# A transformer block on one core: the expert router fed with the sums ahead of the norm, and the second chunk's last norm pass on ScalarE and GpSimd

## The reference, cut to what matters

```python
mix = jnp.concatenate([ret_o, swa_o, mla_o], axis=-1) @ w_out[l]
x = layer_norm(DEEPNORM_ALPHA * x + mix, ln1_g[l], ln1_b[l])
# layer_norm: (xf - mu) * rsqrt(var + LN_EPS) * g + b
ffn = grouped_moe(x, router_w, router_bias, exp_w_gate_up[l], exp_w_down[l])
# grouped_moe: scores = sigmoid(x @ router_w)                      16 experts
#   biased = scores + router_bias; the best of 4 groups (sum of its top 2),
#   then the top 2 experts inside it; gates = their normalised scores
#   h = x @ w_gate_up[e]; a = silu(h[:256]) * h[256:] * gate; y += a @ w_down[e]
x = layer_norm(DEEPNORM_ALPHA * x + ffn, ln2_g[l], ln2_b[l])
```

## Time and profile before

| | us |
|---|---|
| median of 3 runs | 1554.58 (1554.37 to 1555.19) |
| the profiled execution, its own time | 1554.16 |
| its span, first to last instruction | 1552.3 |
| mean granted TensorE clock | 0.998 of full |
| TensorE busy | 1525.1, 98% |
| VectorE busy | 835.7, 54% |
| ScalarE busy | 710.5, 46% |
| POOL busy | 88.8, 6% |

### The profile page before, as it was taken

How to read it: one execution, slowest core, us unless ns; L and a number is a source line. 1 busy time by engine, 2 the same in 40 slices (tenths; PEclk the granted TensorE clock), 3 DMA queues, 4 the chain that set the end, 5 groups by cost and what they waited for, 6 DMA issues and landing times.

```text
span 1552.3 us, 20392 instructions
## 1 busy us (share of the span) xinstructions
PE 1525.1 (98%) x7476; PEld 1167.2 (75%) x7476; DVE 835.7 (54%) x1126; ACT 710.5 (46%) x1179; POOL 88.8 (6%) x159
## 2 busy tenths in 40 slices
PE   8999999999999999999999999999999999999998
PEld 7886445877443788888888888878888888888886
DVE  4675215476422755546667555565555556755544
ACT  5662123674212544446474444453444537554443
POOL 2420000140000000002000000000000010000000
PEclk9999999999999999999999999999999999999999
DMA  7537997546699655566345655546555653655551
GB/s 247 204 135 296 372 421 294 173 142 279 248 421 414 220 184 192 183 207 199 115 156 170 210 191 183 186 152 208 185 185 191 208 164 109 203 190 189 189 189 56
DMA packets 165986, 328.30 MB, mean 211 GB/s; under 512 B 8874, under 2 KB 106896, under 8 KB 152992
## 3 DMA queue, kind: packets, MB, share of 16 engines
q1 hardware_dynamic: 164992, 323.52, 59.5%
q0 software_dynamic: 928, 3.89, 0.8%
HBM read 326.33 MB, written 1.05 MB: 211 GB/s over the span
## 4 chain that ended last, share of the span: by engine, by line
PE 90%; DVE 3%; DMA 3%; ACT 2%; issue 1%; DVEq 1%; POOL 0%; SPq 0%; POOLq 0%; ACTq 0%
PE bank L449 23%; PE bank L451 23%; PE bank L450 23%; PE bank L1221 6%; PE bank L1267 3%; DMA sb_raw<-w_in 2%; PE bank L853 1%; PE bank L1180 1%; PE bank L1181 1%; DMA sb_raw<-ffn_w 1%; PE bank L1275 1%; PE bank L1276 1%; DVE sb_wlo L445 1%; PE bank L930 1%; PE bank L882 1%; ACT sb_whi L438 1%
## 5 line engine op out<-in xcount | busy, mean ns | idle before, releaser
L445 DVE TENSOR_TENSOR sb_wlo<-sb_raw,sb_whi 128x1024 fp32r<-128x1024 f32 (+2 forms) x419 | 483.3, 1197 | 347.4 <-ACT sb_whi L438 347.0
L438 ACT ACTIVATE sb_whi<-sb_raw 128x1024 fp32r<-128x1024 f32 (+2 forms) x419 | 408.0, 1027 | 322.1 <-PE bank L451 303.6
L449 PE MATMUL bank<-sb_whi,sb_op_hi 128*128 128x512 f32 (+2 forms) x1216 | 475.3, 391 | 6.5 <-DVE sb_op_lo L2012 3.5
L451 PE MATMUL bank<-sb_whi,sb_op_lo 128*128 128x512 f32 (+2 forms) x1216 | 467.8, 385 | 0.0
L450 PE MATMUL bank<-sb_wlo,sb_op_hi 128*128 128x512 f32 (+2 forms) x1216 | 467.1, 384 | 0.0
L449 PEld LDWEIGHTS bank<-sb_whi,sb_op_hi 128*128 128x128 f32 x1216 | 228.7, 188 | 53.3 <-issue 4.3
L451 PEld LDWEIGHTS bank<-sb_whi,sb_op_lo 128*128 128x128 f32 x1216 | 228.6, 188 | 46.1
L450 PEld LDWEIGHTS bank<-sb_wlo,sb_op_hi 128*128 128x128 f32 x1216 | 228.9, 188 | 42.6
L449 PE MATMUL bank<-sb_whi,sb_lat_hi 128*128 128x512 f32 (+2 forms) x456 | 175.7, 385 | 1.0 <-DVE sb_wlo L445 1.0
L451 PE MATMUL bank<-sb_whi,sb_lat_lo 128*128 128x512 f32 (+2 forms) x456 | 174.5, 383 | 0.0
L450 PE MATMUL bank<-sb_wlo,sb_lat_hi 128*128 128x512 f32 (+2 forms) x456 | 174.4, 382 | 0.0
(11 more groups left out here) (269 smaller groups left out, 1337.3 us busy)
## 6 DMA issues: line engine op xcount, KB each, us to landing
sb_raw<-ffn_w SPq DMA_DIRECT2D x264, 512.0 KB, 4.3
sb_moe<-exp_w_gate_up SPq DMA_DIRECT2D x46, 1024.0 KB, 9.7
sb_raw<-w_in SPq DMA_DIRECT2D x84, 512.0 KB, 4.6
sb_moe<-exp_w_down SPq DMA_DIRECT2D x26, 1024.0 KB, 10.0
sb_raw<-w_out SPq DMA_DIRECT2D x32, 512.0 KB, 4.4
sb_per_block<-exp_w_gate_up SPq DMA_DIRECT2D x8, 1024.0 KB, 7.0
sb_xT<-exp_w_gate_up SPq DMA_DIRECT2D x6, 1024.0 KB, 10.2
sb_xg<-exp_w_gate_up SPq DMA_DIRECT2D x4, 1024.0 KB, 8.9
```

Of the source, the lines that this page charges most:

```text
L438: nc.scalar.activation(h, r, ACT.Copy).then_inc(hi_made.sem, 1)
L445: nc.vector.tensor_tensor(o, r, h.bitcast(F32), ALU.subtract).then_inc(lo_made.sem, 1)
L449: nc.tensor.matmul(ps, hi, wh, start=first, stop=False)
L451: return nc.tensor.matmul(ps, lo, wh, start=False, stop=last)
```

## The change

- The router no longer reads the normed x. ScalarE copies the four finished sums out of their banks (`sums_out`) into `sums_of` (in the memory that was unused under xs_lo), and TensorE transposes those; chunk 0's transposes stand ahead of the last product group. VectorE's statistics wait for ScalarE's copy of the same half.
- The norm is put into the router weights instead, once in layer 0. With W' = g * W, centred over the 1024 rows, and t = sum of b * W over the rows, the logits are rstd * (sums @ W') + t. g and b of both layers come with the small vectors (two more DMAs, 102 columns in place of 70), VectorE makes the four products and their partial sums, a TensorE matmul with ones adds them over the partitions, and VectorE centres the two weight sets (they lie in `poolw`, which is loaded only in the second model).
- All four copies into xT are ScalarE's. The scaling by rstd and t is two small VectorE operations (`logits`) ahead of the sigmoid.
- The second norm pass of chunk 1 is split: ScalarE multiplies by rstd (`scaled`), POOL adds b. POOL also makes one of the four xs_lo halves. The order of the xs_hi copies, residual matmuls and filler is changed.

```diff
@@ POOL, routing stage @@
                     nc.gpsimd.tensor_tensor(lrstd[:, n % 2:n % 2 + 1], lve[:, n % 2:n % 2 + 1], half[:, 0:1], ALU.pow).then_inc(F["ln_rstd"].sem, 1)
+                    if n == 1:
+                        for nh in range(2):
+                            v, cols_of = x[:, 1, 512 * nh:512 * nh + 512], slice(512 * nh, 512 * nh + 512)
+                            pool.wait_ge(F["normed"].sem, F["normed"].after(l, nh + 1))
+                            nc.gpsimd.tensor_tensor(v, v, table[:, 1, cols_of], ALU.add).then_inc(F["ln1"].sem, 1)
+                        pool.wait_ge(F["xs_hi"].sem, F["xs_hi"].after(l, 1))
+                        lo, hi = (t[:, 0, 4:8, :] for t in (xs_lo, xs_hi))
+                        v = x[:, 0, 512:1024].rearrange("p (q j) -> p j q", j=4)
+                        nc.gpsimd.tensor_tensor(lo, v, hi.bitcast(F32), ALU.subtract).then_inc(F["xs_lo0"].sem, 1)
@@ TensorE @@
+                if l == 0:
+                    pe.wait_ge(rw_summed.sem, 1)
+                    nc.tensor.matmul(bank[4][:, 0:2 * DEPTH * NE], c("ones"), rw_sums, start=True, stop=True).then_inc(rw_total.sem, 1)
                 for ch in range(NC):
                     for nh in range(2):
                         if ch == 0:
                             slab_ready(num(S1_OUT + 2 + nh))
+                        elif nh == 1:
+                            if l == 0:
+                                pe.wait_ge(rw_centred.sem, 1)
+                            routing_transposes(0)
...
-                routing_transposes(0)
+                routing_transposes(1)
                 router(0)
+                router(1)
+                fold(0)
+                fold(1)
+                wait(F, "ln1", l, 2)
                 open_residual(0)
-                routing_transposes(1)
-                fold(0)
-                router(1)
-                fold(1)
-                open_residual(1)
-                kept_busy(3, 512, const[:, 0:512])
+                wait(F, "ln1", l, 3)
+                open_residual(1, (0,))
+                kept_busy(1, 512, const[:, 0:512])
...
                 count(bank[5][:, 0:NE], ones).then_inc(F["counted"].sem, 1)
-                kept_busy(1, 512, const[:, 0:512], 7)
+                wait(F, "ln1", l, 4)
+                open_residual(1, (1,))
@@ ScalarE @@
                 nc.scalar.preload_act_table(ACT.Sigmoid)
+                sums_out(0, 0)
+                sums_out(0, 1)
+                sums_out(1, 0)
                 routing_out(0)
                 routing_out(1)
+                sums_out(1, 1)
+                routing_out(2)
+                routing_out(3)
                 logit_out(0)
+                logit_out(1)
+                wait(F, "scaled", l, 1)
+                scaled(0)
+                wait(F, "logits", l, 1)
+                nc.scalar.activation(scores, biased, ACT.Sigmoid).then_inc(F["routed"].sem, 1)
+                scaled(1)
+                wait(F, "ln1", l, 2)
                 token_hi(0)
-                routing_out(2)
-                logit_out(1)
-                wait(F, "folded", l, 2)
-                nc.scalar.activation(scores.rearrange("p c e -> p (c e)"), bank[5][:, 0:32], ACT.Sigmoid).then_inc(F["routed"].sem, 1)
+                wait(F, "ln1", l, 4)
                 token_hi(1)
@@ VectorE, start of layer 0 @@
+                    for i, weighed in enumerate((rw_g, rw_b)):
+                        for n in range(DEPTH):
+                            o = COLS + DK * (DEPTH * i + n)
+                            tt(weighed[n], rw_tiles, bank[7][:, o:o + DK].unsqueeze(2).to_broadcast([P, DK, NE]), ALU.mult)
+                    dve.drain()
+                    for n, t in enumerate((*rw_g, *rw_b)):
+                        i = nc.vector.tensor_reduce(rw_sums[:, NE * n:NE * n + NE], t.rearrange("p k e -> p e k"), axis=AX.X, op=ALU.add)
+                    i.then_inc(rw_summed.sem, 1)
@@ VectorE, routing stage @@
+                if l == 0:
+                    dve.wait_ge(rw_total.sem, 1)
+                    for n in range(DEPTH):
+                        stt(out=rw_g[n], in0=bank[4][:, NE * n:NE * n + NE].unsqueeze(1).to_broadcast([P, DK, NE]), scalar=-1.0 / D, in1=rw_g[n],
+                            op0=ALU.mult, op1=ALU.add)
+                    nc.vector.tensor_copy(tails, bank[4][:, DEPTH * NE:2 * DEPTH * NE]).then_inc(rw_centred.sem, 1)
+                def logits():
+                    dve.sem_inc(F["scaled"].sem, 1)
+                    wait(F, "folded", l, 2)
+                    for ch in range(NC):
+                        i = stt(out=biased[:, ch, :], in0=bank[5][:, NE * ch:NE * ch + NE], scalar=lrstd[:, ch:ch + 1],
+                                in1=tails[:, NE * l:NE * l + NE], op0=ALU.mult, op1=ALU.add)
+                    i.then_inc(F["logits"].sem, 1)
...
-                wait(F, "opT", l, 8)
-                nc.vector.tensor_copy(xT[:, 4:8, P:T], bank[7][:, :].rearrange("p (k t) -> p k t", k=4)).then_inc(F["xT_d"].sem, 1)
-                token_lo(0, 0)
-                token_lo(0, 1)
...
                     op0=ALU.is_lt, op1=ALU.mult).then_inc(F["hot"].sem, 1)
+                token_lo(0, 0)
                 wait(F, "ranked", l, 1)
```

More of the change, by code:

```diff
@@ L396, in program @@
             ("mix_c0", 2, 0), ("ln_var", 4, 0), ("ln_rstd", 4, 0), ("ln1", 4, 0), ("table", 64, 0),
-            ("xT_a", 3, 0), ("xT_d", 1, 0), ("logit", 8, 0), ("logit_out", 2, 0), ("folded", 2, 0), ("routed", 1, 0),
-            ("hot", 1, 0), ("counted", 1, 0), ("ranked", 1, 0), ("sized", 1, 0), ("in_slot", 4, 0), ("xs_hi", 2, 0), ("xs_lo", 4, 0),
+            ("sums_out", 4, 0), ("xT_a", 4, 0), ("logit", 8, 0), ("logit_out", 2, 0), ("folded", 2, 0), ("scaled", 1, 0), ("normed", 2, 0), ("logits", 1, 0), ("routed", 1, 0),
+            ("hot", 1, 0), ("counted", 1, 0), ("ranked", 1, 0), ("sized", 1, 0), ("in_slot", 4, 0), ("xs_hi", 2, 0), ("xs_lo0", 1, 0), ("xs_lo", 3, 0),
             ("gathered", 2 * DK, 0), ("xg_a", 4, 0), ("xg_d", 12, 0), ("gates", 1, 0), ("slot", PAIRS, 0), ("of_slot", PAIRS, 0),
@@ L1123, in _, with routing_transposes @@
                 slab(num(S1_OUT + 1), (S1_OUT + 1) % RING, 512, range(4), lambda ch: ybank(ch, 1)[:, :], False, False)
+                if l == 0:
+                    pe.wait_ge(rw_summed.sem, 1)
+                    nc.tensor.matmul(bank[4][:, 0:2 * DEPTH * NE], c("ones"), rw_sums, start=True, stop=True).then_inc(rw_total.sem, 1)
+                def routing_transposes(ch, halves_of=range(2)):
+                    for h in halves_of:
+                        wait(F, "sums_out", l, 2 * ch + h + 1)
+                        for k in range(4):
+                            i = nc.tensor.transpose(bank[4 + 2 * ch + h][:, k * P:k * P + P], by_k(sums_of[:, ch, :])[:, 4 * h + k, :], ident)
+                        i.then_inc(F["opT"].sem, 1)
                 for ch in range(NC):
@@ L1132, in _ @@
                         i.then_inc(F["mix_c0"].sem if ch == 0 else slab_done.sem, 1)
[L1134 to L1139, removed]
                 def router(ch):
@@ L1143, in router @@
                         if k % 4 == 0:
[L1144 removed]
+                            wait(F, "xT_a", l, 2 * ch + k // 4 + 1)
                         r = slice(32 * (k % 4), 32 * (k % 4) + 32)
[L1146 removed]
+                        i = nc.tensor.matmul(bank[4 + 2 * ch][r, 0:P], rw_of[l][:, NE * k:NE * k + 32], xT[:, k, ch * P:ch * P + P], start=k < 4, stop=k >= 4)
                         if k >= 4:
@@ L1183, in early_gather @@
                 def early_gather():
-                    wait(F, "xs_lo", l, 2)
+                    wait(F, "xs_lo0", l, 1)
+                    wait(F, "xs_lo", l, 1)
                     wait(F, "in_slot", l, 1)
@@ L1187, in early_gather @@
                         gather(0, k, gather_bank(k), 0)
-                    wait(F, "xs_lo", l, 3)
+                    wait(F, "xs_lo", l, 2)
                     wait(F, "in_slot", l, 2)
@@ L1191, in early_gather @@
                         gather(0, k, gather_bank(k), 1).then_inc(F["gathered"].sem, 1)
-                    wait(F, "xs_lo", l, 4)
+                    wait(F, "xs_lo", l, 3)
                     for k, (name, n) in zip(range(4, DK), (("xg_a", 1), ("xg_d", 1), ("xg_a", 2), ("xg_a", 3))):
@@ L2180, in _, with layer_norm @@
                 lo1(l, 17)
-                def layer_norm(n0, there, done, between=None):
+                def layer_norm(n0, there, done, between=None, last=None):
                     wait(F, "table", l, 16 * (n0 + 2))
@@ L2200, in layer_norm @@
                         wait(F, "ln_rstd", l, n0 + ch + 1)
+                        if ch and last is not None:
+                            last()
+                            break
                         for nh in range(2):
```

39 lines of the change are left out of this document (26 added, 13 removed).

## The result

The changed kernel takes 1559.45 us (median of 11 runs, 1558.47 to 1561.83); the kernel before, run beside it, 1554.68. The ratio is 1.0029, 95% interval 1.0021 to 1.0037. A second set of the same kernel on another occasion gave 1.0036 (1.0022 to 1.0049). The forecast was 1555.2 us in a range of 1549.4 to 1558.6: the time lies 0.85 us above the range.

What follows compares the result with a forecast made beforehand. TensorE, busy 98% of the span, was taken as the bound, with time to gain only in the routing stage's waits. 2 x 0.25 + 0.15 = +0.65 us on the profiled execution gave 1555.2 us, range 1549.4 to 1558.6.

Steps and rivals of the forecast that it cites:

- Step 1: Routing stage: with the router ahead of the norm, the ranking could start 2.15 us earlier.
- Step 2: Routing stage: with work taken from VectorE and nothing in the way, the gather comes 2.6 us earlier per layer.
- Step 3: Ranking: POOL's three instructions hold VectorE's small operations 2.85 us (0 to 4.3), making the gather 0.25 us later per layer.
- Step 4: Set-up in layer 0: VectorE's 2.0 us of extra work is hidden; a ones matmul on TensorE's path costs 0.15 us.
- the sum: Whole kernel: 0.25 us later per layer plus 0.15 for set-up, +0.65 us in all, giving 1555.2 us.
- rival B: Before the gather: holds are real and TensorE's idling drops its clock, up to 1.5 us per layer, 1558.2 us; chance 0.23.
- Rival A: Ranking: POOL does not hold the small VectorE operations, so 5.05 us less, 1549.5 us; chance 0.32.
- Rival C: Program start: the set-up is not hidden and costs 2.0 us, 1557.2 us; chance 0.05.

Runs made afterwards that it cites:

- the four faster kernels: Changed kernel without GpSimd's and ScalarE's part, gaps filled (0.9981); with ranking operands in PSUM (0.9978); that plus filler (0.9976); that plus xs_lo half back on VectorE (0.9977).
- the set-up alone: The kernel before plus only the changed kernel's set-up (loads, products, sums, ones matmul, centring), results unused: 1556.05 us, ratio 1.0001.
- the filled one: The changed kernel with four 512-column filler matmuls instead of one ahead of TensorE's wait for the ranking: 1558.76 us, ratio 1.0018 to the kernel before.
- the PSUM version: The changed kernel, GpSimd's work kept, with one operand of each pair in VectorE's ranking read from PSUM: 1552.87 us, ratio 0.9978 to the kernel before.

## Why the prediction missed

- **Step 1** was right. From the first latent product to the ranking's start it was 92.26 us, now 90.16 and 90.13 in the two profiles: 2.1 earlier, 2.15 forecast. The two new VectorE operations took 0.38 (0.3 taken).
- **Step 2** was right as the bound on hot: without GpSimd beside it the ranking takes 3.5 us (3.28 forecast, 0.30 of it a pause), and that version, with its gaps filled, is faster than before by 2.6 us. Its premise that a microsecond at the gather counts in full did not hold. From layer 0's first expert product to layer 1's norm statistics it is 224.61 us before and 225.25 to 226.44 in the profiles of the four faster kernels, so 0.6 to 1.8 us of layer 0's gain was not kept there.
- **Step 3**, the holds: right in kind, place and number, a little small in size. Forecast 0.85 + 1.05 + 0.95 = 2.85, measured 1.07 + 0.98 + 1.02 = 3.07. The GpSimd additions took 1.28 (1.28 estimated), its xs_lo half 1.53 (1.3). Hot came 1.18 us later than before against the same start (0.71 forecast): 0.22 of the difference is the holds, 0.29 a pause of VectorE ahead of L2303. The first gather was 0.93 us late in layer 0, where 0.25 was forecast.
- **Step 4** was right as far as can be told: no run shows a cost of the set-up clear of noise. From the first latent product to the first finished sum it took 0.16 us more, as the matmul with ones was forecast (0.15); in the profile of the set-up alone it is 0.5.
- **The failed step is the clock, which the sum put at nothing: the choice between the forecast and rival B.** B said that TensorE would stand idle for 3.3 us and the clock fall. It had the right wait (3.38 and 3.14 measured) and the right place, and was given 0.23, while the forecast without it got 0.40. The trace of before had one such wait, 2.62 us, and a fall behind it; a wait that my own sum made longer than that deserved the larger chance. The fall struck in both layers of both profiles. The threshold that I read from that one row ("from an idle time like that 2.62 on", so that a slightly shorter wait would avoid it) was wrong as well: the clock fell behind waits of 2.36 and 2.14 us in one run, and behind 1.76 and 1.54 in another, in layer 0 with a wait of 0.44 after it.
- **The clock's size was off too.** I took 1.5 us a layer. By the table the second profile lost 2.6 and 3.3 us a layer against the filled one, the first 1.0 and 2.4. I priced 3 us of work at half speed; in layer 1 of the first profile the rows are long from 395.02 to about 400.7, over 5 us. Why it lasts longer there is not shown.
- **The sum.** Against the forecast of +0.65 us the filled profile shows +1.0 in the two layers, so that in the profile nearly all but the clock is as forecast. The medians are less kind: with filler the kernel is 2.8 us (1.4 to 4.2) slower than before. The clock's part of the loss of 0.0029 is then 0.0011 with overlapping intervals, and some 2 us beside it are not in my sum; no profile shows what they are.
- **Rival A** (small operations not held) is refuted by every profile in which GpSimd works beside a ranking with all operands in SBUF. **Rival C** (2.0 us for the set-up) lies outside the interval of the set-up run.

## What to carry to other kernels

Work moved to GpSimd beside a chain of short VectorE operations cost that chain here nearly a whole GpSimd instruction at each turn, so move it only where VectorE is in long operations, or give the short ones an operand in PSUM: the same three GpSimd instructions then held none of the short ones, and a kernel 0.29% slower became one 0.22% faster. Whoever shortens or removes filler must see that the wait behind it stays short, since waits of 1.8 and 0.4 us a layer cost 3.1 us over two layers in the medians; filler that overshoots costs what it overshoots. A profile's first 40 us varied by 1.5 us from one execution to the next: compare stretches between like rows, not spans. And see where the profiled execution lies among the others: three of the profiles here are of the fastest one of their kernel.

## What the runs showed that I had not expected

- A VectorE instruction with a single SBUF input, the 128x8 TENSOR_SCALAR, was held as well: 0.82 for 0.17 us. With that input in PSUM it took 0.17 beside GpSimd's second addition. The ranking's reductions were held in none of these profiles. The Trainium skill, SBUF — State Buffer, section Who interferes with whom, names tensor_scalar among the operations that can contend with GpSimd by taking both ports, and tensor_reduce on this chip as one that never does; these rows agree.
- An instruction held by GpSimd ends 0.03 to 0.15 us behind GpSimd's row, whatever its own length: 1.25, 1.27 and 1.21 us for work of 0.18, 0.29 and 0.19.
- Waits of 1.76 and 0.44 us cost the clock in the profile of one kernel and not in that of another, and by the mean clocks in some executions of one kernel and not in others. 0.82 and 0.4 (first filler run) did not; 0.57 and 0.44 did in layer 0 of the PSUM version, 0.35 and 0.41 in its layer 1 did not.
